# Two chunks of the second up unit by seven block products, in a fused transformer trunk

## What is computed

```python
h = rmsnorm(x, norm_mlp[l])
x = x + jnp.square(jax.nn.relu(h @ w_up[l])) @ w_down[l]      # w_up: 2048 x 8192, w_down: 8192 x 2048
```

## Time and profile before

| | |
|---|---|
| median of 3 runs | 2674.16 us (2673.42 to 2676.18) |
| the profiled execution | 2673.84 us, of which the span 2672.1 us |
| TensorE matmuls busy | 2657.7 us (99%) |
| VectorE busy | 2058.7 us (77%) |
| ScalarE busy | 1445.5 us (54%) |
| GpSimd busy | 127.6 us (5%) |
| HBM | 215 GB/s over the span, q1 (SyncE's queue) 61.3% of the 16 engines |
| chunk loads, issue to landing | 4.2 us (median) |

### The profile page before, as it was taken

One profiled execution on the slowest core, in us unless ns is written; L12 is line 12 of the kernel. 1 busy time (PEld: TensorE's weight loads), 2 busy tenths in 40 slices (PEclk: granted clock), 3 DMA queues, 4 the chain that ended last, 5 costly groups with the idle time before them and its releaser, 6 DMA issues.

```text
span 2672.1 us, 37287 instructions
## 1 busy us (share of the span) xinstructions
PE 2657.7 (99%) x13576; PEld 2232.1 (84%) x13576; DVE 2058.7 (77%) x3051; ACT 1445.5 (54%) x1863; POOL 127.6 (5%) x218
## 2 busy tenths in 40 slices
PE   9999999999999999999999999999999999999998
PEld 7788778888888888888888887788888888888887
DVE  5676568977898897987756755689678988989875
ACT  5545555545565555645445455555456556556554
POOL 0100000000100100100010000000001001000000
PEclk9999999999999999999999999999999999999999
DMA  7885545676775766766687655466677767667574
GB/s 259 235 238 169 178 162 187 225 238 236 236 232 194 238 219 208 240 205 236 227 234 227 219 175 172 161 200 225 228 252 234 229 205 239 209 218 233 190 248 152
DMA packets 179961, 575.56 MB, mean 215 GB/s; under 512 B 23016, under 2 KB 43028, under 8 KB 179664
## 3 DMA queue, kind: packets, MB, share of 16 engines
q1 hardware_dynamic: 166256, 536.94, 61.3%
q0 software_dynamic: 13008, 35.98, 5.1%
q10 hardware_dynamic: 528, 0.37, 0.1%
HBM read 535.15 MB, written 38.04 MB: 215 GB/s over the span
## 4 chain that ended last, share of the span: by engine, by line
PE 92%; DVE 4%; DMA 2%; ACT 1%; issue 1%; SPq 0%; POOLq 0%; POOL 0%; ACTq 0%
PE acc L527 24%; PE acc L529 23%; PE acc L528 23%; PE att L495 2%; PE att L497 2%; PE att L496 2%; PE acc L495 2%; PE acc L497 2%; PE acc L496 2%; PE acc L544 1%; PE acc L543 1%; PE acc L545 1%; DVE w_lo L1311 1%; DMA raw<-in_w_main 1%; DVE w_lo L1332 1%; PE turn L496 1%
## 5 line engine op out<-in xcount | busy, mean ns | idle before, releaser
L1311 DVE TENSOR_TENSOR w_lo<-raw,w_hi 128x1024 fp32r<-128x1024 f32 (+1 forms) x778 | 934.8, 1212 | 410.9 <-ACT w_hi L886 409.0
L886 ACT ACTIVATE w_hi<-raw 128x1024 fp32r<-128x1024 f32 (+1 forms) x778 | 813.4, 1051 | 655.8 <-PE acc L529 485.9
L527 PE MATMUL acc<-w_hi,h_hl 128*128 128x512 f32 x1848 | 736.2, 398 | 0.4 <-DVE w_lo L1311 0.3
L529 PE MATMUL acc<-w_hi,h_hl 128*128 128x512 f32 x1848 | 729.0, 394 | 0.0
L528 PE MATMUL acc<-w_lo,h_hl 128*128 128x512 f32 x1848 | 728.5, 394 | 0.0
L527 PEld LDWEIGHTS acc<-w_hi,h_hl 128*128 128x128 f32 x1848 | 347.9, 188 | 82.7 <-issue 4.6
L529 PEld LDWEIGHTS acc<-w_hi,h_hl 128*128 128x128 f32 x1848 | 347.9, 188 | 81.3
L528 PEld LDWEIGHTS acc<-w_lo,h_hl 128*128 128x128 f32 x1848 | 348.3, 188 | 76.0
L1332 DVE TENSOR_TENSOR w_lo<-raw,w_hi 128x1792 fp32r<-128x1792 f32 x166 | 335.5, 2021 | 38.7 <-ACT w_hi L895 37.8
L527 PE MATMUL acc<-w_hi,o_hl 128*128 128x512 f32 x912 | 360.9, 396 | 0.0
L528 PE MATMUL acc<-w_lo,o_hl 128*128 128x512 f32 x912 | 359.9, 395 | 0.0
(11 more groups left out here) (298 smaller groups left out, 3504.7 us busy)
## 6 DMA issues: line engine op xcount, KB each, us to landing
raw<-in_w_main SPq DMA_DIRECT2D x928, 512.0 KB, 4.2
scratch<-spread SPq DMA_DIRECT2D x37, 512.0 KB, 2.7
moved<-scratch SPq DMA_DIRECT2D x148, 128.0 KB, 3.2
scratch<-spread POOLq DMA_DIRECT2D x30, 512.0 KB, 3.6
moved<-scratch POOLq DMA_DIRECT2D x120, 128.0 KB, 4.9
raw<-in_w_misc SPq DMA_DIRECT2D x16, 336.0 KB, 4.4
bias_b<-bias_rows POOLq DMA_DIRECT2D x32, 96.0 KB, 5.7
xs<-in_x SPq DMA_DIRECT2D x4, 512.0 KB, 7.2
```

The source lines that it names most:

```text
L527: nc.tensor.matmul(o, a_hi, hi[:, kk], start=(k == 0), stop=False)
L529: last = nc.tensor.matmul(o, a_lo, hi[:, kk], start=False, stop=fin)
L886: nc.scalar.activation(w_hi[s][:, 0:2 * width], raw[r][:, 0:2 * width], ACT.Copy).then_inc(hi_ready, 1)
L1311: nc.vector.tensor_tensor(w_lo[s][:, 0:2 * width], raw[r][:, 0:2 * width], w_hi[s][:, 0:2 * width].bitcast(F32), ALU.subtract).then_inc(lo ...
```

## The change

The second up unit of each group (up 1) does two chunks by seven products: chunks 5 and 7 in the first group (`WIDE_FIRST`, since the sums of h are not ready earlier), chunks 1 and 3 in the other three. So up 1 needs its sides combined: `take_up(g, 1)` becomes `take_side`, `add_up_sides` and `take_summed`. It uses the second pair of side banks (`SIDES_OF_UP`), and `add_up_sides` picks its accumulators by the unit's number. The first block of each group (`u_moved(g, 0)`) is taken at the end of unit up 1 and not after chunk 2 of unit up 2. The three loops `Fori` over groups become Python loops, so that the program is written out.

```diff
-WIDE_UP = ((1, 3, 5), (), (1, 3, 5, 7), ())
+WIDE_UP = ((1, 3, 5), (1, 3), (1, 3, 5, 7), ())
+WIDE_FIRST = (5, 7)
+SIDES_OF_UP = (0, 1, 0)
...
 # SyncE
-                with sp.Fori(0, GROUPS - 1) as g:
+                for g in range(GROUPS - 1):
...
 # TensorE
-                up(C_MLP + 8, 1, adds(0, 0), 1)
+                up(C_MLP + 8, 1, adds(0, 0), 1, [(c, h_sums_took, (G_SUMS + H_SUMS) * l + G_SUMS + c // 2 + 1) for c in WIDE_FIRST],
+                   WIDE_FIRST)
...
-                    up(g * 64 + (C_MLP + 72), 1, adds(g, 3), 1)
+                    up(g * 64 + (C_MLP + 72), 1, adds(g, 3), 1, wide=WIDE_UP[1])
...
 # ScalarE
-                run(C_MLP + 8, {3: lambda: take_up(0, 0, base + 8, 0)}, {1: lambda: h_sums(3)})
-                with act.Fori(0, GROUPS - 1) as g:
+                run(C_MLP + 8, {3: lambda: take_up(0, 0, base + 8, 0)}, {1: lambda: h_sums(3), 7: lambda: u_moved(0, 0)},
+                    WIDE_FIRST, steps_at(0, -len(WIDE_FIRST)))
+                for g in range(GROUPS - 1):
                     end = g * 64 + base
-                    run(g * 64 + (C_MLP + 16), {5: lambda: take_up(g, 1, end + 16, 1)},
-                        {2: lambda: u_moved(g, 0), 7: lambda: u_sums_hi(g, 0)}, WIDE_UP[2], steps_at(g, AT_UP2))
-                    run(g * 64 + (C_MLP + 24), {4: lambda: take_side(g, 2, end + 24), 7: lambda: take_summed(g, 2, sides_count(g, 0))},
+                    run(g * 64 + (C_MLP + 16), {3: lambda: take_side(g, 1, end + 16), 6: lambda: take_summed(g, 1, sides_count(g, 0))},
+                        {0: lambda: u_sums_hi(g, 0)}, WIDE_UP[2], steps_at(g, AT_UP2))
+                    run(g * 64 + (C_MLP + 24), {4: lambda: take_side(g, 2, end + 24), 7: lambda: take_summed(g, 2, sides_count(g, 1))},
...
-                    run(g * 64 + (C_MLP + 72))
+                    run(g * 64 + (C_MLP + 72), (), {7: lambda: u_moved(g, 4)}, WIDE_UP[1], steps_at(g, AT_UP1))
                 g, end = GROUPS - 1, base + 64 * (GROUPS - 1)
-                run(C_MLP + 64 * g + 16, {3: lambda: take_up(g, 1, end + 16, 1)}, {2: lambda: u_moved(g, 0)},
-                    WIDE_UP[2], steps_at(g, AT_UP2))
+                run(C_MLP + 64 * g + 16, {3: lambda: take_side(g, 1, end + 16), 4: lambda: take_summed(g, 1, sides_count(g, 0))},
+                    (), WIDE_UP[2], steps_at(g, AT_UP2))
...
 # VectorE
-                run(C_MLP + 8, {2: factors}, {1: lambda: h_sums(3), 3: lambda: spread_u(0, 0)})
-                with dve.Fori(0, GROUPS - 1) as g:
+                run(C_MLP + 8, {2: factors}, {1: lambda: h_sums(3), 3: lambda: spread_u(0, 0), 7: lambda: u_moved(0, 0)},
+                    WIDE_FIRST, steps_at(0, -len(WIDE_FIRST)))
+                for g in range(GROUPS - 1):
                     end = g * 64 + base
                     run(g * 64 + (C_MLP + 16), (),
-                        {2: lambda: u_moved(g, 0), 4: lambda: spread_u(g, 1), 7: lambda: u_sums_lo(g, 0)}, WIDE_UP[2], steps_at(g, AT_UP2))
+                        {1: lambda: u_sums_lo(g, 0), 3: lambda: add_up_sides(g, 1, NBLK), 6: lambda: spread_u(g, 1)},
+                        WIDE_UP[2], steps_at(g, AT_UP2))
...
-                    run(g * 64 + (C_MLP + 72), (), {5: lambda: take_down(g, 3, end + 72)})
+                    run(g * 64 + (C_MLP + 72), (), {5: lambda: take_down(g, 3, end + 72), 7: lambda: u_moved(g, 4, g < GROUPS - 2)},
+                        WIDE_UP[1], steps_at(g, AT_UP1))
                 g = GROUPS - 1
-                run(C_MLP + 64 * g + 16, (), {2: lambda: u_moved(g, 0, False), 3: lambda: spread_u(g, 1)},
+                run(C_MLP + 64 * g + 16, (), {3: lambda: add_up_sides(g, 1, NBLK), 4: lambda: spread_u(g, 1)},
                     WIDE_UP[2], steps_at(g, AT_UP2))
```

More of the change, by code:

```diff
@@ L84 @@
 WIDE_AT = tuple(AT_DOWN + sum(len(w) for w in WIDE[:n]) for n in range(NBLK))
-N_WIDE = AT_DOWN + sum(len(w) for w in WIDE)
+AT_UP1 = AT_DOWN + sum(len(w) for w in WIDE)
+N_WIDE = AT_UP1 + len(WIDE_UP[1])
 WIDE_GATE = (1, 3, 5, 7)
@@ L827, in up @@
                     unit(l * CHUNKS + at, 8, h_lhs, acc[bank], None, before, hold=hold, wide=wide, sum_of=h_sum,
-                         sides=wide_acc[n // 2])
+                         sides=wide_acc[SIDES_OF_UP[n]] if wide else None)
                 def down(at, bank, before, n, hold=(), wide=()):
@@ L1220, in steps_at @@
                 def steps_at(g, first):
-                    return lambda i: g * (3 * N_WIDE) + 3 * (l * LAYER_WIDE + GATES_WIDE + first + i + 1)
+                    return lambda i: g * (3 * N_WIDE) + 3 * (l * LAYER_WIDE + MLP_WIDE + first + i + 1)
                 def run(at_chunk, at=(), then=(), wide=(), steps=None):
@@ L1698, in add_up_sides @@
                 def add_up_sides(g, n, i):
-                    z, w = wide_acc[n // 2]
-                    at = g * 2 + (l * LAYER_SIDES + i)
-                    steps = g * 6 + 3 * (l * LAYER_SIDES + i)
+                    z, w = wide_acc[SIDES_OF_UP[n]]
+                    bank = acc[n % 2]
+                    at = g * GROUP_SIDES + (l * LAYER_SIDES + i)
+                    steps = g * (3 * GROUP_SIDES) + 3 * (l * LAYER_SIDES + i)
                     quarters = stage[:].rearrange("p t (h c) -> p (t h) c", h=2)
@@ L1843, in steps_at @@
                 def steps_at(g, first):
-                    return lambda i: g * (3 * N_WIDE) + 3 * (l * LAYER_WIDE + GATES_WIDE + first + i)
+                    return lambda i: g * (3 * N_WIDE) + 3 * (l * LAYER_WIDE + MLP_WIDE + first + i)
                 def run(at_chunk, at=(), then=(), wide=(), steps=None):
@@ L1866, in first_sums_and_spread @@
                         spread_u(g, 2)
-                    run(g * 64 + (C_MLP + 24), {3: lambda: add_up_sides(g, 2, NBLK), 5: lambda: u_moved(g, 1)},
+                    run(g * 64 + (C_MLP + 24), {3: lambda: add_up_sides(g, 2, NBLK + 1), 5: lambda: u_moved(g, 1)},
                         {7: first_sums_and_spread})
```

22 lines of the change are left out of this document (12 added, 10 removed).

## The result

The changed kernel takes **2693.53 us** (median of 6 runs, 2689.71 to 2699.22) against 2674.38 us (6 runs, 2672.67 to 2676.18) on the same chip: ratio **1.0072**, 95% interval 1.0061 to 1.0082, so 19 us slower. The forecast was 2685.8 with a range of 2674 to 2694: right in sign, 8 us too low, and just inside the range. The runs of the changed kernel spread over 9.5 us and those of the kernel before over 3.5. Its profiled execution took 2694.0 us, 20.2 more than that of before.

A forecast was written before the change was run, and what follows sets the result against it. TensorE was taken to bound the whole MLP, with nothing there waiting. Terms -4.8 + 8.5 + 4.2 + 2.3 + 1.8 = +12.0 us on the profiled 2673.84 gave 2685.8 us; range 2674 to 2694.

The forecast's parts named there:

- the clock rival: First group's up 2: idle TensorE drops to the lower clock for two chunks per layer, +11.2 us, 2693 us; chance 0.14.
- The products: 16 new seven-product chunks in up 1, each 0.30 us shorter on TensorE: 4.8 us less in all.
- Step 1: First group's up 2, both layers: TensorE waits 3.2 and 5.3 us for the early-taken first block, 8.5 us more.
- landing + 5.8: First group's up 2: TensorE can begin 5.8 us after the first block lands, behind ACT's copy and DVE's work.
- Step 2: Chunk 4 of the first group's up 2: DVE without lead makes TensorE wait 2.1 us per layer, 4.2 in all.
- my third rival: Same as the clock rival: lower clock for two chunks per layer in place of the chunk 4 wait, 2693 us; chance 0.14.
- my first rival: First group's first block lands early, within 9.3 and 8.2 us of its store; DVE keeps its lead: 2669.0 us; chance 0.10.
- Step 3: Last group's up 2: ACT squares ahead of chunk 4, TensorE waits 2.3 us in two layers, plus 1.8 for later chunks.
- 0.9 per layer: Last group: allowance for chunks 5 and 6 of up 2 and chunk 4 of the next unit, 1.8 us in all.
- Step 4: Two middle groups, up 2: lead of 0.9 us at chunk 4, so nothing lost; end 0.9 us in each of four units.

The follow-up runs named there:

- the early block alone: Kernel before with loops written out and only the first group's first block taken at the end of up 1, no new seven-product chunk: ratio 1.0047 to the kernel before.
- fillers: Changed kernel with 11 matmuls of 512 columns, result overwritten, put on TensorE ahead of unit up 2 of the first group: ratio 1.0056 to the kernel before.

## Why the prediction was right, and where it was short

The direction and the places were right: every new wait that it named came, but for the one at chunk 4 of the first group, which the low clock stood in for. That the time lies inside the range is in part luck. The sum's own ends were 2679 and 2691; 2693.5 is past them and inside only because the range had been drawn to 2694 for the clock rival. The clock did fall, but in the first group it cost no more than the wait that it stood in for. The 8 us that were missing lay elsewhere, in the last group and in units to which I had given nothing.

- **The products, -4.8.** Right: 2.48 to 2.51 us for each of the new chunks, all unit times agree with 0.30.
- **Step 1, 8.5 forecast, 5.9 measured** (2.6 + 3.3). The mechanism is as described, and the term is mis-sized in the landing: I took 12.5 and 13.5 after the store, and ACT took the block after 11.7 and 11.6. My formula landing + 5.8 gives 691.8 and 2027.4; TensorE began at 692.10 and 2027.65. It also gives the two starts of the early block alone (taken at 686.12 and 2022.10, started at 692.17 and 2028.15).
- **Step 2, 4.2 forecast, 4.9 measured, but by another way.** I forecast a wait at chunk 4; there was 0.4 and nothing. The clock fell, chunk 0 took 4.43 and 5.26 us instead of 2.79, and DVE caught up meanwhile. That is my third rival in its mechanism: the low clock stands in the place of step 2, as that rival said, but at 1.6 and 2.8 us instead of 5.6 a layer, since it was low for 3.4 and 6.8 us where two whole chunks at that level take 11.2. I had said that no row and no run shows the lower level. The trace of before does have it, at the very end: 0.50 in its last 4.9 us (2667.20 to 2672.10), with no matmul since 2663.8.
  With the clock held up by fillers the forecast wait is there: 1.8 to 1.9 against 2.1. But my condition for it was wrong. "If step 1 did not happen, this would not either" is refuted twice: with the first block back behind chunk 2 there is no wait ahead of up 2 to speak of and 2.6 us at chunk 4, and with few bytes for all blocks 0.3 at most ahead of up 2 and 1.8 at chunk 4. I had left out that the seven-product chunks of up 1 use DVE's lead by themselves (5.8 and 4.6 us at chunk 0 before, 0.5 and 0.2 with them and without the early block). So my first rival has a wrong step too: in that last run the block landed 8.9 and 6.8 us after its store, inside the rival's 9.3 and 8.2, and DVE did not keep its lead. The rest of the sums is 0.69 in the earlier trace rows and not 0.65, and the pair costs DVE 4.7 and not 4.6; neither changes the step.
- **Step 3, 4.1 forecast, 9.0 measured.** Chunk 4 of the last group's up 2 waits as forecast (row below: 1.18 us by the starts, forecast 1.15), and chunks 5 to 7 begin another 0.6 late.

```profile
1222.57 0.50 PE L532 MATMUL acc<-w_hi,h_hl 128*128 128x512 f32 x1 [1.03 <-DVE w_lo L1318]
```

  What failed is "0.9 per layer ... on them, ends 0 and 2" for all that is behind. The transpose of block 1 was later by the sides, ACT reached its taker one unit on before it landed, and the low clock followed in the first layer:

```profile
1237.85 1.06 ACT L959 ACTIVATE o_hl<-moved 128x1024 fp32r<-128x1024 f32 x1 [5.07 <-DMA moved<-scratch]
```

```profile
1244.07 0.50 PE L532 MATMUL acc<-w_hi,h_hl 128*128 128x512 f32 x1 [1.84 <-DVE w_lo L1318]
```

  The wait of one unit on is 2.0 us by the starts in the first layer and 0.8 in the second. I had worked out this very chain for block 0 and not for block 1.
- **Step 4, nothing forecast.** Right for the units it named: up 2 of both middle groups has no wait, with 0.88 of lead against 0.9 forecast. Wrong as a sum: units further on, where later blocks are taken or chunk loads run beside them, lose 3.8 us in all. The run with few bytes for all blocks has 0.3 us or less in each of them, so these are the blocks' way.
- **The sum.** +12.0 forecast, +20.2 measured: -2.6 in step 1, +0.7 in step 2, +4.9 in step 3, +3.5 in step 4 and other units, +1.6 outside the MLP, the last of which no run ties to the change.

What stays open is why the way of one and the same block differs by 3 us from kernel to kernel, how much of that differs between two executions of one kernel, and which load it is behind. No version tried beats the kernel before. The later sides were tried only with few bytes, and not together with a plain last group.
